# Two down projections of the first block: the input's two halves as one product of 512 columns

## The chip, the cores and the metric

The kernel runs on one core of one Trainium2 chip. The metric is device time in microseconds, the median of the runs shown. Engines are named as in the profile: PE is TensorE's matmul, PEld its weight load, DVE is VectorE, ACT is ScalarE, POOL is GpSimd, SP is SyncE.

## The reference, cut to what matters

Two blocks follow each other on 256 tokens of width 1024. The first has two layers, each with a mixer and a feed-forward part; the change touches the down projection of that feed-forward part, once in each layer:

```python
D_MODEL, SEQ, DEPTH, D_FF = 1024, 256, 2, 2752
for l in range(DEPTH):
    ...                                     # mixer; x = x + ... @ w_out[l]
    h = rmsnorm(x, ffn_norm_w[l])
    u = causal_dwconv(h @ ffn_w_up[l], ffn_conv_w[l], ffn_conv_b[l])
    gate, val = jnp.split(u, 2, axis=-1)
    x = x + (jax.nn.silu(gate) * val) @ ffn_w_down[l]   # [256, 2752] @ [2752, 1024]
```

The second block (four feed-forward parts, latent attention, sliding attention, and a modulation vector from a 1024 x 18432 product) is not touched, but its modulation weights are streamed and multiplied on VectorE beside the first block's work.

## The kernel before, in words

Everything is held transposed, features on the 128 partitions and tokens along the free dimension. All big products are made in float32 by splitting: each weight panel and each input is written as a high part (rounded to the type fp32r) and a low part (the rest), and a product is three matmuls, high by high, high weight by low input, low weight by high input. The helper `mm3` (lines 482 to 487) issues these three; `mm` (line 479, whose call on line 480 is what the profile shows) issues one, so nearly all PE work stands under line 480.

A down projection has 22 tiles of 128 features inside and 8 output tiles of 128. Its weights come as 16 panels of 128 x 1408: panel n holds the first (n even) or second (n odd) eleven inner tiles of output tile m = n // 2. In `down` of TensorE (line 673) a panel is 11 calls of `mm3` with 256 columns, 33 matmuls, all summed into columns 0 to 255 of bank 4 + m % 2. The input's halves are `f_hi` and `f_lo`, each 22 x 256 columns, and `f_lo` lies behind `f_hi` in memory.

The panels go through a line of hand-over between engines. SP starts the transfer of a panel into one of four raw slots when that slot is free. ACT (`high`, line 1271) waits until the panel before the last is used up (semaphore `panels_used`), and writes the high part `w_hi`; DVE (`low`, line 1936) waits for that and writes the low part `w_lo`; PE's `panel` (line 489) waits for the low part. There are two slots of `w_hi` and `w_lo`, so panel n + 2 can be split only when PE has finished panel n, and it has the time of panel n + 1 for that.

DVE works its own program in order (`sweep`, line 1984, and the `body` functions). In step n of a down projection it does: for odd n, wait until panel n is used up and add the tile to the residual, `res = bank + res` (`add_tile`, line 2123, and `residual_plain`, line 2114); then `low` of panel n + 2; then, where `MOD_STEPS` (line 88) says so, one chunk of the second block's modulation (`mod_chunk`, line 1955: two multiply-and-sum instructions over 1024 elements, line 1963). In layer 0 chunks stand at steps 0, 2, 4, ..., 12 and 13; in layer 1 at 0, 2, 4 and 6. After each tile ACT squares it for the coming norm (`sq`), and POOL adds the squares up.

Layer 0 is `down` (line 2140). In layer 1 `down_to_streams` (line 2204) does the same with more in it: from step 7 on DVE also scales the context (line 2223) and writes its low part (line 2034), and a reciprocal stands at step 3 (line 2228). `link` makes DVE wait for its own instruction's end before the next one begins.

Of the kernel before, what the change touches and what calls it, by code (L numbers as in the profile page):

```python
# [7 lines left out]
F32R = mybir.dt.float32r  # L8
ALU = mybir.AluOpType
# [3 lines left out]
P = 128  # L13
DM = 1024
KD = DM // P
T = 256
# [25 lines left out]
HALF_FF = 11  # L42
# [173 lines left out]
    return x[:, 0:PANEL].rearrange("p (t k c) -> p t k c", t=2, k=KD)[:, :, i * (KD // 2):(i + 1) * (KD // 2), :]  # L216


def half_slot(name, n):
    return SPLIT_AT[name, n] % HALVES  # L220


def two_blocks(nc, xT, ctxT, params_d, consts_d, weights, out_d):
    ctx = ExitStack()
    with ctx:
        bytes_at = [nc.sbuf_base + 31 & ~31]

        def sb(name, shape, dt=F32, at=None):

            off = bytes_at[0] if at is None else at  # L230
            size = 4 * int(np.prod(shape[1:])) + 31 & ~31
            if at is None:
                bytes_at[0] += size
            assert off + size <= nc.sbuf_usable_end, name
            return nc.alloc_sbuf_tensor_at("sb_" + name, shape, dt, offset=off)
# [12 lines left out]
        res = sb("res", [P, KD, 2 * T])  # L248
# [14 lines left out]

        M = bytes_at[0]
        bytes_at[0] += 4 * 22 * 512
        f_hi = sb("f_hi", [P, HALF_FF * 512], F32R, at=M)
        f_lo = sb("f_lo", [P, HALF_FF * 512], F32R, at=M + 4 * HALF_FF * 512)
        mid = sb("mid", [P, 22 * 512], at=M)
        normed_f = sb("normed", [P, KD, 2 * T], at=M)
        first_squares = sb("first_squares", [P, KD, T], at=M + 16384)  # L270
# [46 lines left out]
        bank = [ctx.enter_context(nc.psum_tensor(f"bank{b}", [P, 512], F32)) for b in range(8)]  # L317
# [16 lines left out]
        U, at = region(0, U_TILES, UW)  # L334
        xc, at = region(at, 8, T)
        xdt, at = region(at, 2, INNER)
        yss = U[:, 0:4, PAD:UW]
        nsa_y = U[:, 4:6, PAD:UW]
        krq, at = region(at, 4, T)
        tm, at = region(at, 2, TM)  # L340
        acsT, at = region(at, T)
        nPCT, at = region(at, 2, P)
# [3 lines left out]
        key_rope, at = region(6 * 512, 512)  # L346
        pairs = []
        for _ in range(2):
            qn, at = region(at, 2, 512)
            qr, at = region(at, 512)  # L350
            qrot, at = region(at, T)
            kn, at = region(at, 2, 512)
            vv, at = region(at, 4, T)
# [5 lines left out]
        sq_q, at = region(KD * 2 * T, 8, T)  # L359
        sq_qrot, at = region(at, 8, T)  # L360
        sq_k, at = region(at, SWA_KV, 512)
        sq_v, at = region(at, 4, T)
# [26 lines left out]
        def hidden(half, N):  # L389

            return half[:, :].rearrange("p (n t) -> p n t", t=N)

        def mod(l, c, k, s):
            q = (l * N_MOD + c) * KD + k
            return modT[:, q, s:s + 1]
# [79 lines left out]
        def _(pe):  # L475
# [6 lines left out]
            def mm3(out, w, x, start, stop):  # L482

                (wh, wl), (xh, xl) = w, x
                mm(out, wh, xh, start, False)
                mm(out, wh, xl, False, False)
                return mm(out, wl, xh, False, stop)

            def panel(name, n):

                pe.wait_ge(S("raw_free"), RAW_AT[name, n] + 1 + RAW)
                slot = half_slot(name, n)
                return w_hi[slot], w_lo[slot]
# [18 lines left out]
            def both(pair, *index):  # L512
                return tuple(x[index] for x in pair)

            def cols(w, a, n=P):
                return both(w, slice(None), slice(a, a + n))
# [156 lines left out]
            def down(name, N, mid_base):  # L673


                b = take("res_done", KD)
                f = [hidden(x, N) for x in (f_hi, f_lo)]
                per = 2 * T // N

                for n in range(KD * per):  # L680
                    w = panel(name, n)
                    m, part = n // per, n % per
                    if part == 0 and m >= 2:

                        pe.wait_ge(S("res_done"), b + m - 1)
                    for k in range(HALF_FF):
                        if n < per and k in (0, HALF_FF - 2, HALF_FF - 1):
                            pe.wait_ge(S("ff_mid"), mid_base + part * HALF_FF + (k + 1 if k else HALF_FF - 2))
                        last = mm3(bank[4 + m % 2][:, 0:N], cols(w, k * P),
                                   both(f, slice(None), part * HALF_FF + k),  # L690
                                   part == 0 and k == 0, part == per - 1 and k == HALF_FF - 1)
                    last.then_inc(S("panels_used"), 1)

            def up(name, count, N, sem, ready=None, first=0):
# [329 lines left out]
            for i, n in ((2, 1), (3, 3)):  # L1024
                w = panel("mla_down", n)
                pe.wait_ge(S("lat_evac"), i - 1)
                for t in range(2 if n < 3 else 1):
                    for k in range(KD):
                        last = mm3(bank[2 * (i % 2) + t][:, :], cols(w, (t * KD + k) * P), both(h, slice(None), k),
                                   k == 0, k == KD - 1)  # L1030
# [897 lines left out]
        def _(dve):  # L1928
# [4 lines left out]
            def panel_done(name, n):  # L1933
                dve.wait_ge(S("panels_used"), SPLIT_AT[name, n] + 1)
# [188 lines left out]
            def add_tile(k, N, gate_of, at=None):  # L2123
                b = 4 + k % 2
                ins = residual_mod(k, b, *gate_of, N) if gate_of else residual_plain(k, (at(k) if at else bank[b])[:, 0:N])
                ins.then_inc(S("res_done"), 1)

            def project(name, N, after, gate_of=None, at=None):
# [8 lines left out]

                sweep(name, KD // 2, body, after, defer=True)

            def down(name, N, after, gate_of=None, last=True):  # L2140
                per = 2 * T // N

                def body(n, ahead):
                    if n % per == per - 1:
                        panel_done(name, n)
                        add_tile(n // per, N, gate_of)
                    ahead()

                sweep(name, KD * per, body, after, defer=last)
# [54 lines left out]
            def down_to_streams(name, after):  # L2204


                b = take("norm_high", 2 * KD)
                take("norm_split", 2 * KD)
                c = take("rms_done", 3)
                gains = (N_MOD * 0 + 1) * KD  # L2210

                def split_low(n):
                    k, at = n % KD, slice(T, 2 * T) if n < KD else slice(0, T)
                    dve.wait_ge(S("norm_high"), b + n + 1)
                    input_low(ctx_scaled(k) if n < KD else normed_f[:, k, at], h_wide, k, at, mod(0, 0, k, 1 if n < KD else 0))

                def body(n, ahead):
                    if n % 2:
                        panel_done(name, n)
                        add_tile(n // 2, T, None)  # L2220
                    if 7 <= n < 7 + KD:
                        k = n - 7
                        V.scalar_tensor_tensor(ctx_scaled(k), res[:, k, T:2 * T], mod(0, 1, k, 1), rstd[:, T:2 * T], ALU.mult,
                                               ALU.mult).then_inc(S("norm_scaled"), 1)
                    ahead()
                    if n == 3:
                        dve.wait_ge(S("rms_done"), c + 1)
                        link(V.reciprocal(rstd[:, T:2 * T], rstd[:, T:2 * T]))
                    if n == 6:
                        mod_gain(0, 0)  # L2230
                        link(V.tensor_tensor(first_gain[:, :], par("final1"), modT[:, gains:gains + KD, 0], ALU.mult))
                    if 8 <= n < 8 + KD:
                        split_low(n - 8)

                dve.wait_ge(S("ctx_in"), 16)
                sweep(name, 2 * KD, body, after, defer=True)
                dve.wait_ge(S("first_copy"), 1)
                V.scalar_tensor_tensor(rstd[:, 0:T], bank[7][:, 0:T], EPS, rstd[:, 0:T], ALU.mult,
                                       ALU.add).then_inc(S("first_mix"), 1)
                low(after, 1)  # L2240
                dve.wait_ge(S("rms_done"), c + 2)
                link(V.reciprocal(rstd[:, 0:T], rstd[:, 0:T]))
                for n in range(KD + 2):
                    if n < KD:
                        V.scalar_tensor_tensor(normed_f[:, n, 0:T], res[:, n, 0:T], first_gain[:, n:n + 1], rstd[:, 0:T],
                                               ALU.mult, ALU.mult).then_inc(S("norm_scaled"), 1)
                    if n >= 2:
                        split_low(KD + n - 2)
                dve.wait_ge(S("rms_done"), c + 3)
                link(V.reciprocal(rstd[:, T:2 * T], rstd[:, T:2 * T]))  # L2250
                for k in range(KD):
                    V.scalar_tensor_tensor(res[:, k, 0:T], res[:, k, 0:T], par("final1", k, k + 1), rstd[:, T:2 * T],
                                           ALU.mult, ALU.mult).then_inc(S("final1"), 1)
                dve.wait_ge(S("final1"), KD)
# [755 lines left out]
```

## Time and profile before

| | |
|---|---|
| median of 3 runs | 2351.22 us (2349.45 to 2352.1) |
| the profiled execution's own time | 2349.99 us |
| its span | 2348.2 us |
| PE busy | 2276.4 us, 97% of the span, 14536 matmuls |
| DVE busy | 1699.1 us, 72% |
| ACT busy | 951.9 us, 41% |
| POOL busy | 113.9 us, 5% |
| mean granted clock of TensorE | 0.995 |
| down projections of the first block in the trace | 280.3 to 347 us and about 616 to 683 us |

A row of the timeline is a start, a duration, engine, line and instruction. A matmul's duration runs past the start of the next one, because matmuls overlap; the time that PE needs for one in a stream is the distance of two starts. A wait stands in square brackets behind an instruction, with the engine and line whose work ended it.

### The profile page before, as it was taken

Reading aid. Unit: us, or ns where it says so; the run is one execution under the profiler, and the core shown is the slowest. Engines: PE = TensorE matmul, PEld = TensorE weight load, DVE = VectorE, ACT = ScalarE, POOL = GpSimd, SP = SyncE. Lnnn points to the kernel's source line nnn. Section 1 sums busy time; section 2 is a strip of 40 time slices with the busy share of each in tenths; the row PEclk is TensorE's granted clock in tenths of the full one; section 3 lists DMA queues with packets and bytes.
Section 4 is the critical chain, followed back from the end, with each engine's and each line's share of the span. In section 5 each row is a group of like instructions: output and inputs, shape, how many; then the busy total and the mean of one; then the engine's idle time right before and its main releaser. Section 6 shows DMA issues by size and latency. Waiting matters only on the chain.

```text
span 2348.2 us, 35474 instructions
## 1 busy us (share of the span) xinstructions
PE 2276.4 (97%) x14536; PEld 2024.6 (86%) x14536; DVE 1699.1 (72%) x2772; ACT 951.9 (41%) x1410; POOL 113.9 (5%) x77
## 2 busy tenths in 40 slices
PE   7999999899999999999989999999999999999998
PEld 6889988799998888888768888888988888979998
DVE  6789978889989858845444884784895673696774
ACT  4766635766552222235543212212422222475333
POOL 0010010010010000010001000001000001001001
PEclk9999999999999999999999999999999999999999
DMA  6434475345545545532111454454354353313543
GB/s 254 162 144 181 153 265 186 133 180 181 166 174 194 186 149 188 185 116 95 37 72 36 161 188 142 161 180 146 124 201 161 132 176 106 137 52 121 183 154 118
DMA packets 66562, 356.92 MB, mean 152 GB/s; under 512 B 7136, under 2 KB 10208, under 8 KB 42080
## 3 DMA queue, kind: packets, MB, share of 16 engines
q1 hardware_dynamic: 66400, 354.65, 43.2%
q8 instruction: 115, 1.88, 0.3%
q14 instruction: 47, 0.39, 0.0%
HBM read 353.57 MB, written 1.05 MB: 151 GB/s over the span
## 4 chain that ended last, share of the span: by engine, by line
PE 86%; DVE 8%; ACT 4%; issue 1%; DMA 0%; DVEq 0%; SPq 0%; ACTq 0%
PE bank L480 85%; DVE sb_w_lo L1941 3%; ACT sb_w_hi L1266 2%; DVE sb_products L1963 1%; PE bank L1232 1%; ACT sb_nP L1266 0%; DVE sb_latP L2700 0%; DVE sb_rstd L2011 0%; ACT sb_latP L1266 0%; ACT sb_latPT L1266 0%; DVE sb_nP L2545 0%; ACT sb_mid L1266 0%; DMA sb_res<-x 0%; PE bank L1119 0%; ACT sb_decays L1266 0%
## 5 line engine op out<-in xcount | busy, mean ns | idle before, releaser
L1941 DVE TENSOR_TENSOR sb_w_lo<-sb_raw,sb_w_hi 128x2048 fp32r<-128x2048 f32 (+2 forms) x282 | 570.9, 2024 | 149.3 <-ACT sb_w_hi L1266 146.2
L1266 ACT ACTIVATE sb_w_hi<-sb_raw 128x2048 fp32r<-128x2048 f32 (+3 forms) x296 | 493.5, 1669 | 392.5 <-PE bank L480 390.0
L480 PE MATMUL bank<-sb_h_hi,sb_w_hi 128*128 128x512 f32 (+1 forms) x1400 | 510.4, 365 | 2.0 <-DVE sb_w_lo L1941 1.7
L480 PE MATMUL bank<-sb_h_lo,sb_w_hi 128*128 128x512 f32 (+1 forms) x1400 | 507.3, 362 | 0.0
L480 PE MATMUL bank<-sb_h_hi,sb_w_lo 128*128 128x512 f32 (+1 forms) x1400 | 507.2, 362 | 0.0
L1963 DVE CUSTOM_DVE_ANT_0 sb_products<-sb_raw,sb_cond,sb_params 128x1024 f32<-128x1024 f32 x284 | 365.1, 1286 | 33.4 <-DVEq L1965 16.9
L480 PE MATMUL bank<-sb_f_hi,sb_w_hi 128*128 128x256 f32 (+1 forms) x1122 | 368.2, 328 | 4.3 <-DVE sb_w_lo L1941 3.9
L480 PE MATMUL bank<-sb_f_lo,sb_w_hi 128*128 128x256 f32 (+1 forms) x1122 | 366.4, 327 | 0.0
L480 PE MATMUL bank<-sb_f_hi,sb_w_lo 128*128 128x256 f32 (+1 forms) x1122 | 366.4, 327 | 0.0
L480 PEld LDWEIGHTS bank<-sb_h_hi,sb_w_hi 128*128 128x128 f32 x1400 | 264.1, 189 | 44.7 <-DVE sb_w_lo L1941 2.3
L480 PEld LDWEIGHTS bank<-sb_h_hi,sb_w_lo 128*128 128x128 f32 x1400 | 264.1, 189 | 41.2
L480 PEld LDWEIGHTS bank<-sb_h_lo,sb_w_hi 128*128 128x128 f32 x1400 | 264.2, 189 | 41.1 <-issue 0.5
L480 PE MATMUL bank<-sb_raw_hi,sb_w_lo 128*128 128x256 f32 (+1 forms) x924 | 261.1, 283 | 0.0
L480 PE MATMUL bank<-sb_raw_hi,sb_w_hi 128*128 128x256 f32 (+1 forms) x924 | 260.8, 282 | 0.0
L480 PE MATMUL bank<-sb_raw_lo,sb_w_hi 128*128 128x256 f32 (+1 forms) x924 | 260.5, 282 | 0.0
L1266 ACT ACTIVATE sb_sil<-bank 128x512 f32<-128x512 f32 x66 | 39.5, 599 | 530.2 <-PE bank L480 530.2
L480 PEld LDWEIGHTS bank<-sb_f_hi,sb_w_hi 128*128 128x128 f32 x1122 | 213.2, 190 | 24.5 <-DVE sb_w_lo L1941 6.4
L480 PEld LDWEIGHTS bank<-sb_f_hi,sb_w_lo 128*128 128x128 f32 x1122 | 213.3, 190 | 18.2
L480 PEld LDWEIGHTS bank<-sb_f_lo,sb_w_hi 128*128 128x128 f32 x1122 | 213.3, 190 | 18.2
L468 POOL TENSOR_TENSOR sb_sq_sum<-sb_sq,sb_sq_sum 128x256 f32<-128x256 f32 (+1 forms) x68 | 113.2, 1664 | 2219.2 <-ACT sb_sq L1266 2218.9
L2119 DVE SCALAR_TENSOR_TENSOR sb_res<-bank,sb_modT,sb_res 128x256 f32<-128x256 f32 x112 | 49.8, 480 | 174.5 <-PE bank L480 174.0
L480 PEld LDWEIGHTS bank<-sb_raw_hi,sb_w_hi 128*128 128x128 f32 x924 | 175.0, 189 | 0.3 <-issue 0.2
(305 smaller groups left out, 3264.9 us busy)
## 6 DMA issues: line engine op xcount, KB each, us to landing
sb_raw<-w_mod SPq DMA_DIRECT2D x144, 512.0 KB, 3.2
sb_raw<-w_l_up SPq DMA_DIRECT2D x44, 1024.0 KB, 4.8
sb_raw<-w_l_in SPq DMA_DIRECT2D x26, 1024.0 KB, 6.0
sb_raw<-w_l_down SPq DMA_DIRECT2D x32, 704.0 KB, 4.2
sb_raw<-w_m0a_up SPq DMA_DIRECT2D x22, 1024.0 KB, 4.8
sb_raw<-w_m0b_up SPq DMA_DIRECT2D x22, 1024.0 KB, 4.8
sb_raw<-w_m1a_up SPq DMA_DIRECT2D x22, 1024.0 KB, 4.8
sb_raw<-w_m1b_up SPq DMA_DIRECT2D x22, 1024.0 KB, 4.8
```

The costliest lines, as they stand in the source:

```text
L468: nc.gpsimd.tensor_tensor(sq_sum[:, a:b], sq[:, k % 2, a:b], sq_sum[:, a:b], ALU.add).then_inc(S("sq_added"), 1)
L480: return nc.tensor.matmul(out, lhsT, rhs, start=start, stop=stop, skip_group_check=True)
L1232: last = nc.tensor.transpose(bank[4 + h2][:, c * P:(c + 1) * P], swP[:, u % 2, h2, c * P:(c + 1) * P], ident)
L1266: return nc.scalar.activation(out, in_, func, **kw)
L1941: V.tensor_tensor(split_part(name, n, w_lo[s]), landed_part(name, n, raw[raw_slot(name, n)]), split_part(name, n, w_hi[s]).bitcast(F32), A ...
L1963: link(V.tensor_tensor_reduce(products[:, :], raw[slot][:, 0:DM], cond[:, s, :], 1.0, par("mod_b", g, g + 1), ALU.mult, ALU.add, modT[:, g ...
L2119: last = V.scalar_tensor_tensor(res[:, k, at:at + T], bank[b][:, at:at + T], mod(l, c, k, s), res[:, k, at:at + T], ALU.mult, ALU.add)
```

## The change

For output tiles 0 to 6 of both down projections (seven of eight, 14 of 16 panels each), the two matmuls that use the high weight become one. The input's halves are declared as one tensor `f_pair` of two parts, and one matmul of 512 columns streams first 256 columns of the high half and then 256 columns of the low half against the high weight, into the whole bank. The low weight by the high input stays a matmul of 256 columns, summed into columns 0 to 255. So two partial sums lie side by side in the bank, and DVE adds each of them to the residual: first columns 256 to 511 (`add_beside`, with `link`), then as before columns 0 to 255. Tile 7 stays as it was. The names `f_hi` and `f_lo` still mean the same memory elsewhere.

```diff
+def pair_tile_of(name, m):
+    return name in ("l0_down", "l1_down") and m < KD - 1
...
-        f_hi = sb("f_hi", [P, HALF_FF * 512], F32R, at=M)
-        f_lo = sb("f_lo", [P, HALF_FF * 512], F32R, at=M + 4 * HALF_FF * 512)
+        f_pair = sb("f_pair", [P, 2, HALF_FF * 512], F32R, at=M)
+        f_hi, f_lo = f_pair[:, 0, :], f_pair[:, 1, :]
...
+            def mm_beside(out, w, pair, start, stop):
+                wh, wl = w
+                mm(out, wh, pair, start, False)
+                return mm(out[:, 0:T], wl, pair[:, 0, :], False, stop)
...
                 f = [hidden(x, N) for x in (f_hi, f_lo)]
+                f_beside = f_pair[:, :, :].rearrange("p a (n t) -> p a n t", t=T)
...
-                        last = mm3(bank[4 + m % 2][:, 0:N], cols(w, k * P),
-                                   both(f, slice(None), part * HALF_FF + k),
-                                   part == 0 and k == 0, part == per - 1 and k == HALF_FF - 1)
+                        at, edges = part * HALF_FF + k, (part == 0 and k == 0, part == per - 1 and k == HALF_FF - 1)
+                        if pair_tile_of(name, m):
+                            last = mm_beside(bank[4 + m % 2][:, :], cols(w, k * P), f_beside[:, :, at, :], *edges)
+                        else:
+                            last = mm3(bank[4 + m % 2][:, 0:N], cols(w, k * P), both(f, slice(None), at), *edges)
...
+            def add_beside(m, gate_of):
+                low_half, out = bank[4 + m % 2][:, T:2 * T], res[:, m, 0:T]
+                if gate_of:
+                    link(V.scalar_tensor_tensor(out, low_half, mod(*gate_of, m, 0), out, ALU.mult, ALU.add))
+                else:
+                    link(V.tensor_tensor(out, low_half, out, ALU.add))
...
                     if n % per == per - 1:
+                        m = n // per
                         panel_done(name, n)
-                        add_tile(n // per, N, gate_of)
+                        if pair_tile_of(name, m):
+                            add_beside(m, gate_of)
+                        add_tile(m, N, gate_of)
...
                     if n % 2:
                         panel_done(name, n)
+                        if pair_tile_of(name, n // 2):
+                            add_beside(n // 2, None)
                         add_tile(n // 2, T, None)
```

## Rows read from the trace of the kernel before

**Rows 1.** The page, part 4: the chain that ended last, by engine.
```profile
PE 86%; DVE 8%; ACT 4%; issue 1%; DMA 0%; DVEq 0%; SPq 0%; ACTq 0%
```

**Rows 2.** The chain through layer 0's down projection: start, duration (us), what.
```profile
302.50 1.39 ACT sb_w_hi L1266
303.91 1.64 DVE sb_w_lo L1941
...
308.79 1.62 DVE sb_w_lo L1941
310.46 8.19 PE bank L480 x66
318.73 1.39 ACT sb_w_hi L1266
...
326.69 8.20 PE bank L480 x66
```

**Rows 3.** Timeline of DVE in layer 0: additions and the low part after one.
```profile
292.56 1.61 DVE L1941 TENSOR_TENSOR sb_w_lo<-sb_raw,sb_w_hi 128x1408 fp32r<-128x1408 f32 x1
...
308.45 0.42 DVE L2115 TENSOR_TENSOR sb_res<-bank,sb_res 128x256 f32<-128x256 f32 x1
...
348.32 0.42 DVE L2115 TENSOR_TENSOR sb_res<-bank,sb_res 128x256 f32<-128x256 f32 x1
```

**Rows 4.** Timeline of PE in layer 0: 256 columns in a stream, and one wait.
```profile
299.72 0.28 PE L480 MATMUL bank<-sb_f_hi,sb_w_hi 128*128 128x256 f32 x1
...
302.72 0.28 PE L480 MATMUL bank<-sb_f_lo,sb_w_hi 128*128 128x256 f32 x1
...
310.04 0.28 PE L480 MATMUL bank<-sb_f_hi,sb_w_lo 128*128 128x256 f32 x1
310.46 0.39 PE L480 MATMUL bank<-sb_f_hi,sb_w_hi 128*128 128x256 f32 x1
310.68 0.28 PE L480 MATMUL bank<-sb_f_lo,sb_w_hi 128*128 128x256 f32 x1
```

**Rows 5.** Timeline of PE in the second block: 512 columns in a stream.
```profile
799.66 0.39 PE L480 MATMUL bank<-sb_h_hi,sb_w_lo 128*128 128x512 f32 x1
...
802.83 0.39 PE L480 MATMUL bank<-sb_h_lo,sb_w_hi 128*128 128x512 f32 x1
```

**Rows 6.** Timeline of DVE: an instruction with `link`, and the next.
```profile
652.20 0.17 DVE L2231 TENSOR_TENSOR sb_first_gain<-sb_params,sb_modT 128x8 f32<-128x8 f32 x1
652.40 0.42 DVE L2115 TENSOR_TENSOR sb_res<-bank,sb_res 128x256 f32<-128x256 f32 x1
```

**Rows 7.** Timeline of ACT in layer 0: the square after the addition.
```profile
308.91 0.42 ACT L1266 ACTIVATE sb_sq<-sb_res 128x256 f32<-128x256 f32 x1 [1.07 <-DVE sb_res L2115]
```

**Rows 8.** The chain through layer 1's down projection.
```profile
647.45 1.63 DVE sb_w_lo L1941
...
653.22 1.54 DVE sb_w_lo L1941
...
654.81 24.03 PE bank L480 x198
...
678.92 1.93 ACT sb_w_hi L1266
...
683.21 16.85 PE bank L480 x128
```

**Rows 9.** Timeline of DVE in layer 1: low part after the reciprocal; a step without a chunk.
```profile
639.59 1.63 DVE L1941 TENSOR_TENSOR sb_w_lo<-sb_raw,sb_w_hi 128x1408 fp32r<-128x1408 f32 x1 [0.73 <-ACT sb_w_hi L1266]
...
667.32 0.48 DVE L2223 SCALAR_TENSOR_TENSOR sb_sil<-sb_res,sb_modT,sb_rstd 128x256 f32<-128x256 f32 x1
...
668.45 1.63 DVE L1941 TENSOR_TENSOR sb_w_lo<-sb_raw,sb_w_hi 128x1408 fp32r<-128x1408 f32 x1 [0.66 <-ACT sb_w_hi L1266]
```

**Rows 10.** After layer 0: us; busy of PE, PEld, DVE, ACT, POOL; clock; DMA; GB/s.
```profile
354.00:357.40 3.40, 3.37 (x16) 3.40 (x17) 3.40 (x10) 1.84 (x5) 0.00 (x0) 0.50 0.00 0
```

**Rows 11.** The page, part 5: weight loads; busy us, mean ns, idle before.
```profile
L480 PEld LDWEIGHTS bank<-sb_f_lo,sb_w_hi 128*128 128x128 f32 x1122 | 213.3, 190 | 18.2
```

## The prediction

> **What bounds the kernel now.** I read the chain that ended last first: 86% of the span is PE, 8% DVE [rows 1], so as a whole PE is the bound and a matmul saved should be time saved. But this is a mean. The chain through the first down projection [rows 2] looks otherwise, and this is what the reader should see: PE holds it for two panels (x66), then ACT, then four steps of DVE, then PE again, and this repeats every 16.23 us (310.46 to 326.69). Layer 0 is bound by a loop of hand-overs in which DVE has the greater part. In layer 1 PE holds the chain for the last six panels without a break (x198) [rows 8]. So the question is what the change does to the loop in layer 0 and to the stream in layer 1. I number panels 0 to 15 and write S for a panel's first matmul.
>
> **What PE saves.** In a stream, 25 matmuls of 256 columns take 299.72 to 302.72, so 0.120 us each [rows 4]; 14 of 512 columns take 799.66 to 802.83, so 0.2264 us each [rows 5]. A panel of 33 x 0.120 = 3.96 us becomes 11 x (0.2264 + 0.120) = 3.81 us. The columns are the same; only the fixed part of one matmul in three goes, 0.15 us a panel. Over 28 panels this is 4.2 us, the most that the change can give. After a wait the first two starts lie 0.22 us apart instead of 0.12 (310.46, 310.68) [rows 4]; a first matmul of 512 columns takes 0.2264 anyway, so I let this 0.10 us vanish too.
>
> The trace shows no matmul whose moving operand is read in two pieces. Below, 0.2264 us is the price with no penalty; above, I take two matmuls of 256, 0.240 us, since nothing here shows a reason why one instruction should cost more than the two it replaces. I take 0.2264, the row with the same number of columns.
>
> On the fixed part, [rows 4, 5] solve to about 13.6 ns (2 x 0.120 minus 0.2264) beside a time per column. The Trainium skill, "TensorE: Matmul & The Clock Gate", section "Wait — 56ns, not 53.3ns?", says that warm back-to-back matmuls are spaced by the columns at 2.4 GHz and only about 2.5 ns more. By that rule a panel would save 0.03 us and not 0.15, the 28 panels 0.8 us and not 4.2, and the sum below would end near +1.6 us. The trace disagrees (it has a weight load before every matmul), and I go by the trace.
>
> **What DVE pays.** The new addition reads 128x256 from the bank as the old one does: 0.42 us [rows 3]. With `link` the next instruction starts about 0.03 us after the end of the linked one (652.20 + 0.17, then 652.40) [rows 6]; without it, additions hand over after 0.34 us (308.45 to 308.79) [rows 2, 3]. So one costs 0.45 us, 14 of them 6.3 us of DVE. Whether it counts depends on what DVE waits for next. Bounds: 0.34 if `link` cost nothing, about 0.60 if a wait on the bank cost as the 0.15 us after the chunks does; small beside the rest. ACT's square starts 0.46 us after the addition and stays clear of the next high part (308.91, moved to 309.4) [rows 7], so ACT and POOL only move.
>
> **Layer 0.** The loop before: high part starts at 302.50, low part 1.41 us later, then the chunk, addition 4.54 us after the low part's start (308.45), next low part 0.34 later, PE 1.67 later: 7.96 us from 302.50 to S7 = 310.46. From there two panels and the hand-over to ACT at 318.73 take 8.27 us: 7.92 of products, 0.10 of the slow start, 0.25 of latency [rows 2 to 4]. Sum 16.23, as seen. After: 7.96 + 0.45 = 8.41, and 2 x 3.81 + 0.25 = 7.87; sum 16.28. What four panels win on PE, 0.35 us, is less than the 0.45 us of the addition in the loop, of which there is one per four panels; the addition on the other pair of panels has slack. So +0.05 us a turn, three turns (S3 to S15): +0.15. Before them, S3 hangs on the addition of tile 0 and the low part at 292.56 [rows 3], both behind the last feed-forward tile's work and a chunk, and PE is already waiting: +0.45, and panels 0 and 1 win nothing, since panel 2 waits for its low part. S15 comes 0.60 us later.
>
> Panel 15 is of tile 7, unchanged. The end is DVE's: low part of 15, the chunk of step 13, the low part of the next stage, the addition at 348.32 [rows 3]; then the norm. All this is DVE's order, so it is later by 0.60 us, and so is the next layer's start. **Layer 0: +0.60 us.**
>
> **Layer 1.** The same start: S3 +0.45. Then the additions of tile 1, and the reciprocal behind them, move 0.72 later (0.45 for tile 1's, 0.27 handed on from tile 0's by way of ACT's squares). DVE sat idle for 0.73 us after the reciprocal, until ACT had the high part for 639.59 [rows 9]: no cost, but with hardly any room. The next addition pair adds 0.45, S7 is about 0.54 late. The low part at 647.45 waits for panel 6, which now ends 0.25 us earlier; from its start to that of the low part at 653.22 [rows 8] come the chunk, two small instructions, the addition and the scaling, plus 0.45: S9 is 0.45 - 0.25 = 0.20 us late. From there no chunk stands in the way. In a step such as that of panel 13 DVE sits idle for 0.66 us before the low part, waiting for ACT, after addition and scaling (667.32, 668.45) [rows 9]; 0.45 us fits in there. So panels 9 to 13 run at PE's pace: 5 x 3.81 = 19.05 instead of 0.10 + 5 x 3.96 = 19.90, 0.85 less. The x198 run and the ACT step after it at 678.92 [rows 8] come 0.85 - 0.20 = 0.65 us earlier, and so do the low part and PE at 683.21. **Layer 1: -0.65 us.**
>
> **Sum.** +0.60 - 0.65 = -0.05, so nothing: 2349.94 against the profiled execution's 2349.99, and 2351.2 against the median of 2351.22. The profiled one lies 1.2 us under that median, the runs shown lie within 2.7 us, so I keep the median.
>
> **The clock** bounds the handing on. PE idles at layer 0's end, and 354.0 to 357.4 runs at a granted 0.50, its 1.2 GHz level, [rows 10]; work of 3.4 us at half speed costs 1.7 us. The change moves work there by half a microsecond. I count nothing and keep up to 1.7 us either way as the bound.
>
> **Rivals.**
> (a) PE's share decides: chunk and addition have more cover than I read, and all 28 panels save 0.15 us: -4.2 us, 2347.0. For it: PE 86% of the chain [rows 1]. Against: the loop in [rows 2], where each figure is a row. Chance 0.10.
> (b) The two-piece operand costs, and the kernel is slower. At 0.240 us a product a panel stays at 3.96: a turn of layer 0 is 16.23 + 0.45, so 0.45 + 3 x 0.45 = +1.80; layer 1 is late at S9 by some 0.96 and wins nothing after: +2.8, 2354.0. From there every further ns counts on the products in the loops and in the stream, about 66 + 33 + 55 = 154 of 308; it passes +4.7 us at 0.240 + 1.9 / 154 = 0.252 us. Nothing in the trace speaks for it, nor can it exclude it. Chance 0.17, 0.04 of it beyond 0.252.
> (c) The change doesn't do what it says: the matmuls become 512 wide but the fixed part stays, because the weight load before each small matmul can't hide behind its neighbour. Weight loads of 0.190 us [rows 11] overlap in a stream of 0.12 us steps, which speaks against. It would be (b)'s 2354.0 at most. Chance 0.05.
> (d) A shifted clock step, 1.7 us either way. Chance 0.08.
> Forecast 0.60, its own range 2349.2 to 2353.0.
>
> **Numbers.** About 0.2%, 4.7 us, is what can be told from no change. The greatest gain, 4.2 us, lies within it, so faster needs (a) and luck beside: 0.03. Slower needs (b) beyond 0.252, or something of this size that I don't see: 0.05. Same 0.92. The range takes in (a) and the first end of (b): 2347.0 to 2354.2.
>
> **What would show it.** PE: distances 0.226 and 0.120 us in turn. Layer 0: turns of about 16.28 us and waits before panels 7, 11 and 15 of about 1.0 us where 0.3 stood, DVE on the chain still. DVE: 14 more additions on the new line, 0.42 us each. Layer 1: panels 9 to 13 every 3.81 us without waits, ACT at 678.92 - 0.65 against the stage's start. It would be wrong if the distance of a two-piece product is not 0.226, if the addition costs clearly more than 0.45, or if DVE no longer reaches ACT's high parts in time in layer 1.

## The result, and the profile after

The changed kernel takes 2353.68 us (median of 20 runs, 2350.08 to 2355.94), the kernel before 2350.07 us (20 runs, 2347.4 to 2353.43). The ratio is 1.0015, interval 1.0008 to 1.0021: slower by 1.9 to 4.9 us where no change was forecast. The profiled execution has a span of 2351.9 us, 3.7 more.

First the page of the changed kernel, part 4, the chain by engine. DVE has two points more of it than in [rows 1], PE two points less: more of the span than before hangs on hand-overs.

```profile
PE 84%; DVE 10%; ACT 4%; issue 1%; DMA 0%; DVEq 0%; SPq 0%; ACTq 0%
```

Then the chain of the changed kernel through one turn of layer 0, which answers to [rows 2] (start, duration, what). It is the same loop with one new link: the row at 308.62 is the new addition (line 2160).

```profile
302.67 1.39 ACT sb_w_hi L1280
...
304.08 1.64 DVE sb_w_lo L1955
...
308.62 0.44 DVE sb_res L2160
...
309.08 0.04 DVE sb_res L2129
...
309.43 1.62 DVE sb_w_lo L1955
...
311.10 8.05 PE bank L485 x44
...
319.23 1.39 ACT sb_w_hi L1280
...
327.65 2.35 PE bank L485 x12
```

From 302.67 to 311.10 are 8.43 us (forecast 8.41), from there to 319.23 are 8.13 (forecast 7.87), and a turn, 311.10 to 327.65, takes 16.55 (forecast 16.28; 16.23 before). So the addition costs what was reckoned, and the two panels of PE cost 0.26 us more than reckoned. PE's own timeline shows why; it answers to [rows 4]:

```profile
309.35 0.39 PE L485 MATMUL bank<-sb_f_pair,sb_w_hi 128*128 128x512 f32 x1
309.58 0.28 PE L485 MATMUL bank<-sb_f_pair,sb_w_lo 128*128 128x256 f32 x1
309.69 0.39 PE L485 MATMUL bank<-sb_f_pair,sb_w_hi 128*128 128x512 f32 x1
309.92 0.28 PE L485 MATMUL bank<-sb_f_pair,sb_w_lo 128*128 128x256 f32 x1
311.10 0.50 PE L485 MATMUL bank<-sb_f_pair,sb_w_hi 128*128 128x512 f32 x1 [0.89 <-DVE sb_w_lo L1955]
311.43 0.28 PE L485 MATMUL bank<-sb_f_pair,sb_w_lo 128*128 128x256 f32 x1
...
673.79 0.40 PE L485 MATMUL bank<-sb_f_pair,sb_w_hi 128*128 128x512 f32 x1
...
676.97 0.40 PE L485 MATMUL bank<-sb_f_pair,sb_w_hi 128*128 128x512 f32 x1
```

After the wait the first two starts lie 0.33 us apart, not 0.23: the slow start of 0.10 us stays. And there are two paces. Near 309 a pair (one matmul of 512 columns and one of 256) takes 0.34 to 0.35 us, from 673.79 to 676.97 nine pairs take 3.18, 0.353 us each. A panel is 3.81 us at the one and 3.89 us at the other.

To see where the 3.7 us of the span lie I cut each trace at four events: DVE's low part of panel 2 in layer 0, the addition of tile 7 there, the low part of panel 2 in layer 1, and the first matmul of the second block. "Middle" is layer 1's mixer and up projection, in which no line was changed; "rest" is all from that matmul to the end. Stretches in us; the medians are of the timed runs. A ratio compares with runs of the kernel before that were made beside that kernel's (their medians lie at 2349.6 to 2350.5 us). It isn't the quotient of two medians, and where runs fall into two groups the two differ.

| kernel | layer 0 | middle | layer 1 | rest | median | ratio to before |
|---|---|---|---|---|---|---|
| before | 60.66 | 274.99 | 59.90 | 1664.99 | 2350.07 | |
| before again (e11) | 60.68 | 274.91 | 59.93 | 1664.94 | | |
| changed | 61.80 | 277.01 | 60.45 | 1665.00 | 2353.68 | 1.0015 [1.0008, 1.0021] |
| changed again (e1) | 61.96 | 276.72 | 60.44 | 1664.82 | 2353.63 | 1.0015 [1.0006, 1.0024] |
| changed again (e12) | 61.94 | 274.91 | 60.08 | 1665.07 | | |
| products only (e2) | 60.12 | 276.54 | 58.89 | 1661.78 | 2346.25 | 0.9985 [0.9976, 0.9994] |
| additions only (e3) | 62.50 | 277.09 | 60.94 | 1664.82 | 2355.58 | 1.0022 [1.0013, 1.0030] |
| low part first (e4) | 65.04 | 274.95 | 63.09 | 1661.64 | 2358.05 | 1.0032 [1.0019, 1.0044] |
| order on DVE and ACT (e5) | 60.23 | 276.65 | 60.09 | 1664.98 | 2351.04 | 1.0001 [0.9993, 1.0010] |
| order without the change (e6) | 60.45 | 274.90 | 60.46 | 1664.70 | 2352.08 | 1.0009 [1.0000, 1.0018] |
| contiguous (e7) | 61.95 | 277.01 | 60.30 | 1662.38 | 2353.47 | 1.0017 [1.0008, 1.0025] |
| covered tiles (e8) | 60.48 | 274.93 | 59.20 | 1661.93 | 2348.73 | 0.9997 [0.9989, 1.0006] |
| delay alone (e9) | 61.93 | 275.99 | 59.93 | 1661.91 | 2353.02 | 1.0013 [1.0004, 1.0022] |
| changed and delay (e10) | 64.45 | 277.12 | 59.93 | 1662.04 | 2355.30 | 1.0025 [1.0016, 1.0035] |
| one early delay (e13) | 63.40 | 275.39 | 59.93 | 1661.75 | 2351.94 | 1.0009 [1.0000, 1.0017] |
| three early delays (e14) | 66.58 | 275.41 | 60.00 | 1661.90 | 2359.97 | 1.0031 [1.0021, 1.0042] |
| covered tiles again (e15) | 60.47 | 275.01 | 59.58 | 1661.95 | 2348.35 | 0.9994 [0.9985, 1.0003] |

The two changed stretches cost +1.1 to +1.3 us and +0.2 to +0.6 us: 1.4 to 1.8 us together. Both unchanged ones come in several sizes, in the middle by 2 us, in the rest by 3 us, in the same code. So does the part ahead of the first event: 287.6 to 290.2 us. All of this goes with TensorE's clock. These are windows of the changed kernel's trace (stretch in us; busy of PE, PEld, DVE, ACT, POOL; granted clock; DMA), then of its third trace (e12), then of the kernel before:

```profile
354.30:361.00 6.70, 5.85 (x27) 5.88 (x28) 6.28 (x17) 3.86 (x9) 0.00 (x0) 0.50 0.00 0
463.50:466.80 3.30, 3.30 (x16) 3.23 (x17) 3.30 (x6) 2.36 (x6) 0.00 (x0) 0.50 0.13 47
```
```profile
354.40:361.10 6.70, 3.35 (x16) 3.38 (x17) 6.67 (x15) 3.02 (x8) 0.00 (x0) 0.50 0.29 124
463.50:470.00 6.50, 5.02 (x50) 4.47 (x51) 6.12 (x14) 5.41 (x8) 0.00 (x0) 1.00 0.37 101
```
```profile
350.70:357.40 6.70, 3.37 (x16) 3.40 (x17) 6.67 (x15) 3.05 (x8) 0.00 (x0) 0.50 0.30 125
463.30:470.00 6.70, 6.03 (x57) 5.35 (x56) 6.39 (x12) 4.18 (x10) 0.00 (x0) 1.00 0.43 157
```

All three have a stretch at 0.50, its 1.2 GHz level, after layer 0. In the first, PE works in 5.85 us of it and is slow again at 463.5; in the second and third PE works in 3.4 us of it and stays at full speed later. The first has a middle of 277.01 us, the second and third 274.91 and 274.99, though the second is the changed kernel too. So 2 us of the profiled difference are the clock's.

The seventeen traces agree in this. The part ahead of the first event is 288.9 to 290.2 us in the twelve that have a 0.50 stretch at 126 to 129 us, and 287.6 to 288.5 us in the five without. The rest is 1664.7 to 1665.1 us in the eight that have a 0.50 stretch of 6.8 us about 17 us behind the one near 1210 us, and 1661.6 to 1662.4 us in the nine that have none there. The middle goes with the distance from layer 0's last addition to the start of the 0.50 stretch behind it. In the fourteen traces where that stretch lasts 6.8 us, a distance of 2.0 to 2.4 us goes with a middle of 274.9 to 275.0 us, 3.2 to 3.3 with 275.4, and 3.7 to 5.1 with 276.5 to 277.1; these last are also the only ones of the fourteen with a second stretch, at 462 to 467 us.

The timed runs show it too, by the mean granted clock of each, which is known to 0.001. In the set of e1 the kernel before takes 2347.6 us at 0.997 (6 runs), 2349.5 at 0.996 (5), 2351.3 at 0.995 (13) and 2352.8 at 0.994 (3). The changed kernel takes 2350.1 at 0.996 (1 run), 2353.5 at 0.995 (5) and 2354.6 at 0.994 (5); neither here nor in its first 20 runs does it reach 0.997. So at the same clock (a step of 0.001 is worth 1.6 to 1.9 us, so this is rough) it is about 2 us slower, near what the two stretches cost, and the remaining 1.3 us of the 3.3 between this set's medians come with a lower clock.

### The profile page after: what moved, and what is told of

It reads as the page before. It is cut to its first block, busy times and chain, and to the rows that moved or that the text cites. A ratio compares the mean times of both kernels' runs of the same rounds, so it can differ in the third digit from the quotient of the medians.

```text
span 2351.9 us, 34872 instructions
## 1 busy us (share of the span) xinstructions
PE 2276.9 (97%) x14228; PEld 2010.5 (85%) x14228; DVE 1705.0 (72%) x2786; ACT 951.5 (40%) x1410; POOL 113.8 (5%) x77
## 3 DMA queue, kind: packets, MB, share of 16 engines
q8 instruction: 112, 1.84, 0.3%
HBM read 353.57 MB, written 1.05 MB: 151 GB/s over the span
## 4 chain that ended last, share of the span: by engine, by line
PE 84%; DVE 10%; ACT 4%; issue 1%; DMA 0%; DVEq 0%; SPq 0%; ACTq 0%
PE bank L485 84%; DVE sb_w_lo L1955 3%; ACT sb_w_hi L1280 2%; DVE sb_products L1977 1%; DVE sb_swS L2822 1%; DVE sb_swP L2836 0%; DVE sb_latP L2727 0%; ACT sb_nP L1280 0%; DVE sb_rstd L2025 0%; ACT sb_latP L1280 0%; DMA sb_raw<-w_l_in 0%; ACT sb_latPT L1280 0%; DVE sb_nP L2572 0%; ACT sb_mid L1280 0%; DVE sb_nP L2599 0%
## 5 line engine op out<-in xcount | busy, mean ns | idle before, releaser
L485 PE MATMUL bank<-sb_f_pair,sb_w_hi 128*128 128x512 f32 (+1 forms) x1936 | 522.0, 353 | 8.3 <-DVE sb_w_lo L1955 8.3
L485 PEld LDWEIGHTS bank<-sb_f_pair,sb_w_hi 128*128 128x128 f32 x1936 | 341.3, 189 | 61.3 <-DVE sb_w_lo L1955 11.5
L485 PE MATMUL bank<-sb_f_pair,sb_w_lo 128*128 128x256 f32 (+1 forms) x1122 | 365.7, 326 | 0.0
L485 PEld LDWEIGHTS bank<-sb_f_pair,sb_w_lo 128*128 128x128 f32 x1122 | 212.4, 189 | 18.2
L485 PEld LDWEIGHTS bank<-sb_raw_lo,sb_w_hi 128*128 128x128 f32 x924 | 174.9, 189 | 0.1
L485 PEld LDWEIGHTS bank<-sb_raw_hi,sb_w_lo 128*128 128x128 f32 x924 | 174.3, 189 | 0.0
```

Source lines behind the costliest of these rows:

```text
L485: return nc.tensor.matmul(out, lhsT, rhs, start=start, stop=stop, skip_group_check=True)
```

## The experiments

Theory "hand-overs": the loss is the addition inside a loop of ACT, DVE and PE. Rivals: the product itself costs, every addition costs wherever it stands, or the clock's stretches are part of the change's price. The edits are cut to what matters; what stands in them behind a # is a note.

**e1, changed again.** No edit.

> The changed kernel once more. Four stretches are read from its trace: layer 0's down projection (low part of panel 2 to the addition of tile 7; 60.66 us before, 61.80 after), the middle (from there to layer 1's low part of panel 2; 274.99 and 277.01), layer 1's (from there to the first matmul of the second block; 59.90 and 60.45), and the rest (1665.0 in both). Theory 'hand-overs': the down projections cost 1.1 and 0.55 us again, to 0.1 us, since they are a fixed order of waits; the middle's 2.0 us are the place where the slow stretches of TensorE's clock fell and may come out anywhere between 275 and 277. Rival 'the clock': the change itself makes TensorE's slow stretches longer, so the middle is 277 again.

Measured: 61.96 and 60.44 us, 0.16 and 0.01 from the first trace (0.1 was expected); middle 276.72. The two stretches' cost repeats. The middle doesn't decide between the two: 276.7 fits both.

**e2, products only.**

```diff
-                        if pair_tile_of(name, m):
-                            add_beside(m, gate_of)
                         add_tile(m, N, gate_of)
...                                                # the same in layer 1
```

> The changed kernel without the new additions: the products stand side by side, the second half of each tile's result is not added (that part of the sum is left out). Theory 'hand-overs': DVE's 0.45 us leave the loop, so a turn of layer 0 is 16.23 - 0.3 = 15.9 to 16.0 us and the stretches are about 60.66 - 0.9 = 59.8 us for layer 0 and 59.90 - 1.0 = 58.9 us for layer 1; median time 1.5 to 2 us under the kernel before. Rival 'the product itself': if the 512-column product is the cost, layer 0 stays above 60.66 without the additions too.

This kernel leaves the second half of each sum out. Measured: 60.12 and 58.89 us, so 0.54 and 1.01 under the kernel before, and a ratio of 0.9985 [0.9976, 0.9994]. Its rest of 1661.78 us is one of the short ones, so as far as its trace tells, only the 1.55 us of the two stages are the products', not all 4 us of its median. Layer 1 is as expected, layer 0 by 0.3 us above it (slow start, slower pace). The products are a gain; the rival "the product itself" falls. DVE's low parts of layer 1 in this run come 3.81 us apart, each after waiting for ACT, so here PE sets the pace:

```profile
670.26 1.63 DVE L1955 TENSOR_TENSOR sb_w_lo<-sb_raw,sb_w_hi 128x1408 fp32r<-128x1408 f32 x1 [0.66 <-ACT sb_w_hi L1280]
674.08 1.63 DVE L1955 TENSOR_TENSOR sb_w_lo<-sb_raw,sb_w_hi 128x1408 fp32r<-128x1408 f32 x1 [0.36 <-ACT sb_w_hi L1280]
```

**e3, additions only.**

```diff
+                        if name == "l0_down" and n // per < KD - 1:
+                            add_again(n // per)        # linked, bank columns 0 to 255
                         add_tile(n // per, N, gate_of)
...                                                # the same in layer 1
```

> The kernel before, with a second linked addition of the same size in front of each of the seven additions (the tile is added twice). Products as before. Theory 'hand-overs': the addition counts four times in layer 0 (S3, S7, S11, S15), 60.66 + 4 x 0.45 = 62.5 us, turns of 16.68 us; in layer 1 it counts to S9, about +0.9 to +1.2, and then is covered: 60.9 us. Rival 'additions are covered, products cost': 60.7 and 59.9 us.

This kernel adds each tile twice. Measured: 62.50 and 60.94 us, both as the theory had them; ratio 1.0022 [1.0013, 1.0030]. Seven additions of 0.45 us cost 1.84 us in layer 0, which is four of them, and about one is lost in each turn. Its low parts in one turn (the second row has no wait before it: DVE's program, not ACT, is late):

```profile
306.87 1.62 DVE L1941 TENSOR_TENSOR sb_w_lo<-sb_raw,sb_w_hi 128x1408 fp32r<-128x1408 f32 x1 [2.33 <-ACT sb_w_hi L1266]
312.21 1.61 DVE L1941 TENSOR_TENSOR sb_w_lo<-sb_raw,sb_w_hi 128x1408 fp32r<-128x1408 f32 x1
...
323.56 1.62 DVE L1941 TENSOR_TENSOR sb_w_lo<-sb_raw,sb_w_hi 128x1408 fp32r<-128x1408 f32 x1 [1.82 <-ACT sb_w_hi L1266]
```

**e4, low part first.**

```diff
...
+                    if low_first(name, n):      # odd n of layer 0, 1, 3, 5 of layer 1
+                        next_low()
                     body(n, ahead)              # additions; then low part (if not yet), chunk
```

> The changed kernel with DVE's order turned: after an odd panel the low part of the panel after the next is made first, then both additions (layer 0 all odd steps but the last, layer 1 steps 1, 3 and 5). Theory 'hand-overs': both additions, 0.79 us, leave the loop; a turn is 16.55 - 0.79 = 15.8 us or less, layer 0 takes about 59.2 us, layer 1 about 59.0 us; median 2 to 3 us under the changed kernel and at or under the kernel before. Rival 'DVE's total': DVE has too much work in these stages whatever the order, so the turn stays at 16.5 us.

Measured: 65.04 and 63.09 us, a miss by 6 and 4 us. Neither theory had this. The chain of this kernel shows a new loop without PE in it:

```profile
307.17 1.64 DVE sb_w_lo L1960
...
311.78 1.63 DVE sb_w_lo L1960
313.40 0.34 DVE sb_res L2171
...
313.77 0.44 DVE sb_res L2140
...
314.55 1.37 ACT sb_w_hi L1285
...
315.95 1.64 DVE sb_w_lo L1960
```

It closes in 8.78 us for two panels (307.17 to 315.95). ACT's program has the square of the tile before the next high part, and the square waits for the additions, which now come after the low part. A step taken out of one engine's path had been the release of another engine's.

**e5, the order turned on both engines**, and **e6, the same without the change.**

```diff
                 def body(n, ahead):              # ACT
                     ahead()                      # high part of panel n + 2
+                    if low_first(name, n - 1):
+                        tile((n - 1) // per)     # square of the tile before
-                    if last and n % per == per - 1:
+                    if last and n % per == per - 1 and not low_first(name, n):
                         tile(n // per)
...                                              # the same in layer 1; DVE's order as in e4, from n = 1 on
```

> The low part first, as in the run before this, and ACT's square of a tile moved behind the next high part. What made the low-part-first kernel slow is by the trace a new loop: addition, then ACT's square, then ACT's next high part, then DVE's low part, 8.78 us for two panels. Theory 'hand-overs': with the square out of that loop and both additions out of the old one, a turn of four panels is about 7.58 + 7.87 + 0.1 = 15.6 us; layer 0 takes 59.2 us (60.66 before, 61.80 changed), layer 1 about 58.8 us (59.90, 60.45). Median 3.5 to 5 us under the changed kernel. Rival 'DVE's total': turns stay above 16.3 us.

> The kernel before with the same two orders (low part first, square behind the next high part), its products and single additions kept. Theory 'hand-overs': the loop is 7.62 + 8.27 = 15.9 us a turn, hardly above PE's own 15.84; layer 0 takes about 59.9 us, layer 1 about 59.5 us. Against the run before this it tells what the products side by side are worth once the addition is out of the loop: 0.5 us in layer 0 and 0.7 us in layer 1 by theory; the rival says nothing or a loss.

Measured: 60.23 and 60.09 us with the change (59.2 and 58.8 were expected), 60.45 and 60.46 without (59.9 and 59.5 expected). A turn of e5 takes 15.95 us, where the rival "DVE's total" had more than 16.3. So the loop of e4 is gone, and with the additions out of the old loop the products side by side are worth 0.22 and 0.37 us, of 0.5 and 0.7 expected. Against the kernel before, the order alone gains 0.2 us in layer 0 and loses 0.6 in layer 1, because something else took the addition's place. (e6's median lies 2.4 us above its kernel before all the same, with ten of its eleven runs at a clock of 0.995.) In e5 the chunk's first instruction takes 1.53 us instead of 1.28 (the last row is POOL's, from the timeline):

```profile
305.07 1.64 DVE sb_w_lo L1964
...
306.84 1.53 DVE sb_products L1986
...
309.93 1.64 DVE sb_w_lo L1964
...
305.42 1.88 POOL L478 TENSOR_TENSOR sb_sq_sum<-sb_sq,sb_sq_sum 128x256 f32<-128x256 f32 x1 [148.46 <-ACT sb_sq L1285]
```

The square now falls so that the chunk starts while POOL's sum of squares runs. The time from one low part to the next is 4.86 us, against 4.88 with the addition between them before. No run took POOL away, but the traces leave little room for another cause. Over all seventeen, 63 chunk instructions start while POOL adds, and each takes 1.53 us or more; of the 4833 others none takes more than 1.29. Of the low parts of 1408 columns, eight start while POOL adds; six of them take 1.73 to 2.01 us, and all others 1.61 to 1.63, also the more than 500 during which POOL starts.

**e7, contiguous.**

```diff
+        f_side = sb("f_side", [P, FF1_TILES, 2, T], F32R, at=M)
...
-                f_beside = f_pair[:, :, :].rearrange("p a (n t) -> p a n t", t=T)
+                f_beside = f_side[:, :, :, :].rearrange("p n a t -> p n (a t)")
```

> The changed kernel with the two halves of each inner tile laid beside each other in memory, so that the 512 columns are one contiguous piece. In the changed kernel's panels the pair of products takes 0.3464 us in some stretches and 0.353 in others. Theory A: the slower pace comes from reading two pieces; here every panel takes 3.81 us, layer 1's low parts from panel 11 on lie 3.81 apart (3.88 in the changed kernel) and layer 1 is at about 60.0 us. Theory B: the pace is a matter of how the engine starts again after a wait; 3.88 us is seen here too, and the stretches stay at 61.8 and 60.4 us within 0.3.

Measured: 61.95 and 60.30 us. Both paces are there with one piece too; its low parts late in layer 1 lie 3.9 us apart:

```profile
672.40 1.63 DVE L1957 TENSOR_TENSOR sb_w_lo<-sb_raw,sb_w_hi 128x1408 fp32r<-128x1408 f32 x1 [0.20 <-ACT sb_w_hi L1282]
676.30 1.63 DVE L1957 TENSOR_TENSOR sb_w_lo<-sb_raw,sb_w_hi 128x1408 fp32r<-128x1408 f32 x1 [0.43 <-ACT sb_w_hi L1282]
```

Theory A falls: reading two pieces costs nothing. In these traces the pace mostly changes at a wait and then holds, which fits theory B; what in the start decides it stays open.

**e8 and e15, covered tiles.**

```diff
-    return name in ("l0_down", "l1_down") and m < KD - 1
+    return (name, m) in {("l0_down", 1), ("l0_down", 3), ("l0_down", 5), ("l1_down", 1), ("l1_down", 4), ("l1_down", 5), ("l1_down", 6)}
```

> The changed kernel with only the tiles paired whose addition is not in the loop: tiles 1, 3 and 5 of layer 0, and 1, 4, 5 and 6 of layer 1. Theory 'hand-overs': no turn gets longer, each holds one paired panel less 0.07 to 0.15 us; layer 0 60.3 us (60.66 before), layer 1 59.3 us (59.90 before); median within 1.5 us under the kernel before. Rival 'each addition costs wherever it stands': 3 x 0.45 us in layer 0 and 4 x 0.45 us in layer 1 less the products' share, 61.5 and 60.7 us.

> The kernel that pairs only tiles 1, 3, 5 of layer 0 and 1, 4, 5, 6 of layer 1, once more. Theory 'hand-overs': layer 0 60.3 to 60.5 us, layer 1 59.2 to 59.5, median 0.5 to 1.5 us under the kernel before, the ratio's interval touching 1. Rival 'chance': the median lies as far above as it lay below in the first run.

The set in this edit pairs tiles 1, 3 and 5 in layer 0 and 1, 4, 5 and 6 in layer 1. Measured: layer 0 60.48 and 60.47 us, layer 1 59.20 and 59.58; 0.18 and 0.3 to 0.7 us under the kernel before. Ratios 0.9997 [0.9989, 1.0006] and 0.9994 [0.9985, 1.0003]: under the changed kernel by 5 us in the median, of which 2.0 to 2.7 us lie in the two stages, and not to be told from the kernel before. The same edit on seven tiles instead of fourteen turns a loss of 1.4 to 1.8 us in the two stages into a gain of 0.5 to 0.9. "Every addition costs" would have given 61.5 and 60.7. This is the best version found; that it beats the kernel before isn't shown by its time.

**e9 to e14, the clock.** What is left of the 3.5 us is about 2. The middle's size goes with where the slow stretch lies, so the question is whether a shift by itself moves the work into the costly place.

```diff
+                        if name == "l0_down" and n == 2 * KD - 1:   # e9, e10; n == 1 in e13, e14
+                            for _ in range(1):                      # 2 in e10, 3 in e14
+                                link(V.tensor_tensor(products[:, :], cond[:, 0, :], cond[:, 1, :], ALU.add))
```

> The kernel before with nothing but one linked DVE instruction of about 1.25 us (into scratch memory) in front of the addition of tile 7 in layer 0: a pure delay there, about as large as the changed kernel's loss in layer 0. In the ten traces so far the middle stretch of the same code is 274.9 to 275.0 us where TensorE's slow stretch begins 2.1 to 2.4 us after that addition, (or 5.5, when it is short) and 276.5 to 277.1 where it begins 3.7 to 5.0 after it. Theory 'clock position': shifting the work by 1.25 us moves it into the costly position in most executions, so the middle is 276.5 to 277.1 and the median rises by 2.5 to 3 us, twice the delay. Rival 'the position is chance': the median rises by 1.25 us.

> The changed kernel with two such instructions, 2.5 us, at the same place. Theory 'clock position': the work is moved on to the next cheap position, the middle falls from 277 to 275 in most executions, and the median rises by 0 to 1 us only. Rival 'the position is chance': the median rises by 2.5 us over the changed kernel's, to about 2356.2.

> The kernel before once more, for its trace. Theory 'clock position': middle stretch 275.0 with the slow stretch beginning 2 to 3 us after the last addition of layer 0. Rival 'the position is chance': 277 is as likely.

> The changed kernel a third time, for its trace. Theory 'clock position': middle stretch 276.5 to 277.1, the slow stretch beginning 3.7 to 5.0 us after the last addition of layer 0. Rival 'the position is chance': 275 is as likely.

> The kernel before with one linked DVE instruction of 1.26 us into scratch memory in step 1 of layer 0's down projection, in front of the addition of tile 0. It makes layer 0 as late as the change does (60.67 + 1.26 = 61.9 us) but leaves the idle time at its end as it was. Theory 'clock position': the median rises by 2.5 to 3.3 us, more than the delay, and where the trace shows the slow stretch 3.7 to 5 us after the last addition, the middle is 276.5 to 277.1. Rival 'the position is chance': the median rises by 1.3 us and no more than 1.8.

> The same with three such instructions, 3.8 us. Theory 'clock position': the positions repeat, after about this much the work is back in the cheap position, so the median rises by 3.3 to 4.5 us, no more than 1.2 us above the run with one instruction, and the middle is 275. Rival 'the position is chance': 3.8 us, 2.5 us above the run with one.

Measured: e9 rises by 0.13% [0.04, 0.22], 3.1 us, for a delay of 1.26 (its median by 3.4). That lies just above the clock's 2.5 to 3 us, but 1.25 is in the interval too, and its middle is 275.99 and not 276.5 or more. e10 lies 1.6 us above the changed kernel by the medians and 2.4 us by the two ratios, for 2.5 us of delay, nearer to chance than to the clock's 0 to 1; its middle is 277.12, where the clock's theory had 275. In both the delay made PE's idle time longer, and the slow stretch lasted 10.2 us instead of 6.8, which I had not foreseen, so they don't decide. e11 and e12 are one execution each. e11 (middle 274.91) fits both. e12 is a changed kernel with a middle of 274.91: against the expectation that it falls in the costly place. Its slow stretch begins 2.3 us after the last addition, so the tie between place and middle holds; where the changed kernel falls isn't fixed. In e13 a slow stretch follows right behind the delay, inside layer 0, and the stage takes 63.40 us, where the delay alone gives 61.93 (e9); the window of its trace (columns as above):

```profile
297.30:300.50 3.20, 3.20 (x17) 3.20 (x16) 3.02 (x4) 0.00 (x0) 0.00 (x0) 0.50 0.91 276
```

By its ratio it rises by 2.1 us [0.0, 4.0], by its median by 1.4; its runs lie in two groups (2350.1 to 2352.1, and three near 2356.3, these at a clock of 0.993). e14 rises by 7.3 us [4.9, 9.9] for 3.8, by its median by 9.4, and also has two groups (2353.4 to 2355.2, and four near 2360.3, these at 0.993), so "no more than 1.2 us above e13" is wrong. The traces of both are of the lower groups. The theory that a shift alone gives the missing 2 us isn't borne out; nor is chance, since the changed kernel's median lay 3.6 and 3.3 us up in sets of 20 and 11 runs. That the missing part goes with the clock is shown; why the changed kernel gets the lower clock more often stays open.

## Why the prediction was wrong

Forecast 2351.2 us, no change; measured 2353.68, inside the range of 2347.0 to 2354.2, but slower beyond its interval. The mechanism stood; the sizes of its terms didn't, and the clock, counted as nothing, came on top.

- **The loop in layer 0** was right as a form: DVE on the chain, four of layer 0's seven additions counting (e3: 1.84 us for 4 x 0.45), tiles 1, 3 and 5 with slack (e8). S3 is 0.46 us later, 0.45 forecast. The stage's +0.60 came out as +1.1 to +1.3.
- **"I let this 0.10 us vanish too"** is the step that failed first. After each wait the first two starts lie 0.33 us apart: 0.2264 + 0.10. It stands in every turn, before and after, and I had struck it from the changed side alone: 0.3 us in layer 0, with three waits, and 0.2 us in layer 1, behind S3 and S9.
- **The product's price** was taken as 0.2264 us from [rows 5]. The distance of a pair is 0.346 or 0.353 us, where the sum had 0.346 throughout. At the slower pace a panel saves 0.07 us, not 0.15. The bound of 0.240 held. My reason for worry, the two pieces, was not the cause (e7). This is the largest of the wrong sizes in the first trace's layer 1: nine panels there run at the slower pace.
- **Layer 1's -0.65** was +0.2 to +0.6. Of the step from panel 8's low part to panel 9's, +0.45 was reckoned and +0.71 came. The low part of panel 8 took 1.87 us instead of 1.62 in all three traces of the changed kernel. It started while POOL added up the squares, as in e5: POOL's sum, behind the additions, came 0.79 us later than before against the stage's start, the low part 0.18. So "ACT and POOL only move" was wrong here: moved, POOL met DVE. The covered part went as said, at 3.89 instead of 3.81 us a panel; in e12, with 3.81, layer 1 is 0.4 us shorter. The first row is DVE's, the second POOL's.

```profile
650.77 1.87 DVE L1955 TENSOR_TENSOR sb_w_lo<-sb_raw,sb_w_hi 128x1408 fp32r<-128x1408 f32 x1 [0.76 <-ACT sb_w_hi L1280]
...
649.41 1.75 POOL L473 TENSOR_TENSOR sb_sq_sum<-sb_sq,sb_sq_sum 128x512 f32<-128x512 f32 x1 [7.29 <-ACT sb_sq L1280]
```

- **The sum** of both stages was -0.05 and is +1.4 to +1.8. For the first trace the same working, with these sizes, gives in layer 0 0.60 + 0.30 for three slow starts + 0.15 for two slow panels in the turns = +1.05, of +1.14 measured. In layer 1 it gives -0.65 + 0.20 for two slow starts + 0.68 for nine slow panels + 0.25 for POOL = +0.48, of +0.55 measured. For e12, with four slow panels in layer 1 instead of nine, it gives +0.10 there, of +0.18 measured.
- **A slip beside it**: "what four panels win on PE, 0.35 us" should be 0.40 for the two panels on the chain (8.27 against 7.87). The sum of 16.28 has it right.
- **The clock** was left out at up to 1.7 us either way. [Rows 10] have one slow stretch; the changed kernel's first trace has another, and 2 us of the span's 3.7 lie in code that didn't change. By the timed runs of e1 the clock is about 1.3 us of the 3.3 between the medians. The term was put at nothing because the work moved by only half a microsecond; it moved by more than one, and that the clock's part came out near its bound, and upward, isn't explained by any run.
- **The rivals.** (a) is excluded by e3. (b) had the right sign and the wrong cause. (c) the fixed part stayed in half, at one of the two paces. (d), the shifted clock step, given 0.08, is what the loss outside the two stages looks like.
- By the Trainium skill's page "TensorE: Matmul & The Clock Gate", section "Wait — 56ns, not 53.3ns?", which has some 2.5 ns fixed for each matmul, e2 would have gained 0.8 us at most on all 28 panels, an estimate. Its two stages are 1.55 us shorter, and a pair at 0.346 us saves 13.6 ns against three matmuls of 0.120. The trace decides.

## What to carry to other kernels

A busy share of 97% doesn't tell what one stage is worth: read the chain there, and count how often an added instruction stands between two hand-overs. Half of the additions here were free and the other half cost more than their products gained, so put such a trade only where the adding engine is seen waiting. Before moving a step out of one engine's path, look for who waits on its semaphore: in e4 this was ACT, at 2.6 to 3.2 us a stage over the changed kernel. And don't strike a start-up cost from one side of a sum only.

## What the hardware showed beside

- Pairs of a 512- and a 256-column matmul run at two paces, 0.346 and 0.353 us, in the same code; the streams of one width looked at showed one pace (0.120 and 0.2264 us, [rows 4, 5]). The pace mostly changes at a wait and then holds; what sets it stays open.
- The first distance after a wait is 0.10 us longer than in the stream, for 256 (0.22) and for 512 columns (0.33), and as much after a wait of 0.2 us as after one of 2: 0.220 to 0.227 us in 58 cases, 0.333 to 0.344 in 83, all at full clock in the two stages.
- A DVE instruction that starts while POOL adds takes longer (1.53 us and more against 1.28 for a chunk's, for a low part, in six of eight cases, 1.73 to 2.01 against 1.62); one during which POOL starts doesn't.
- The same code took 274.9 to 277.1 us in the middle stretch and 1661.6 to 1665.1 in the rest, going with the number and place of the 0.50 stretches of the clock. Runs of one kernel spread over 6 us, in step with their mean clock, so a stage of 60 us that repeats to 0.2 us (0.4 where the pace changes) tells more than a median.
